# A gate map by 384 indirect transfers that add, in place of one-hot matmuls, and down loads eight tiles ahead

## The reference, cut to what matters

```python
v1, i1 = lax.top_k(s1, PEER_TOPK)            # 16 of 128 keys, per frame and head
v2, i2 = lax.top_k(s2, PEER_TOPK)
cand = (v1[..., :, None] + v2[..., None, :]).reshape(N, PEER_HEADS, 256)
cidx = (i1[..., :, None] * PEER_NKEYS + i2[..., None, :]).reshape(N, PEER_HEADS, 256)
sc, sel = lax.top_k(cand, PEER_TOPK)
eidx = jnp.take_along_axis(cidx, sel, axis=-1).reshape(N, 128)
gate = jax.nn.softmax(sc, axis=-1).reshape(N, 128)
...
a = jnp.einsum('nd,ned->ne', xk, u_emb[ek])
coef = jax.nn.gelu(a, approximate=False) * gk
return jnp.einsum('ne,ned->nd', coef, v_emb[ek])
```

## Time and profile before

| | |
|---|---|
| median of 3 runs | 2089.0 us (2085.16 to 2090.39) |
| profiled execution | 2082.26 us, of it the span 2080.4 us |
| mean granted TensorE clock | 0.962 |
| TensorE matmuls | 1855.5 us busy (89%) |
| VectorE, ScalarE, GpSimd | 1183.3, 667.3, 529.1 us busy |
| DMA | 337.63 MB, mean 162 GB/s |

### The profile page before, as it was taken

How to read it: one execution, slowest core, us unless ns; L and a number is a source line. 1 busy time by engine, 2 the same in 40 slices (tenths; PEclk the granted TensorE clock), 3 DMA queues, 4 the chain that set the end, 5 groups by cost and what they waited for, 6 DMA issues and landing times. The chain is left out here.

```text
span 2080.4 us, 24469 instructions
## 1 busy us (share of the span) xinstructions
PE 1855.5 (89%) x8991; PEld 1498.2 (72%) x8991; DVE 1183.3 (57%) x2275; ACT 667.3 (32%) x1004; POOL 529.1 (25%) x422
## 2 busy tenths in 40 slices
PE   5999999889995899999999999996987777888776
PEld 4867777667884788888888888885865655666655
DVE  3269746436999688882222223346755565665656
ACT  4332123333322246663222222331322222222223
POOL 4643200004444400000000000037643333334330
PEclk9999979999998999999999999998999999999998
DMA  4322100412332339898444454557767767777773
GB/s 136 91 61 65 44 1 1 160 43 86 97 92 86 103 96 234 212 237 224 150 141 146 142 153 144 184 210 245 268 237 250 250 238 259 249 254 262 253 256 130
DMA packets 241691, 337.63 MB, mean 162 GB/s; under 512 B 119857, under 2 KB 178609, under 8 KB 241473
## 3 DMA queue, kind: packets, MB, share of 16 engines
q1 hardware_dynamic: 219088, 269.60, 41.9%
q0 software_dynamic: 22528, 67.19, 9.7%
HBM read 282.19 MB, written 54.53 MB: 162 GB/s over the span
## 5 line engine op out<-in xcount | busy, mean ns | idle before, releaser
L344 PE MATMUL psum<-v_hi,c_hi 128*128 128x512 f32 x768 | 318.0, 414 | 125.5 <-DVE c_lo L1682 125.5
L344 PE MATMUL psum<-x_hi,ts_hi_u 128*128 128x512 f32 x1024 | 406.0, 396 | 22.2 <-DVE ts_lo_u L1157 18.9
L345 PE MATMUL psum<-x_lo,ts_hi_u 128*128 128x512 f32 x1024 | 402.2, 393 | 0.0
L346 PE MATMUL psum<-x_hi,ts_lo_u 128*128 128x512 f32 x1024 | 402.0, 393 | 0.0
L1919 POOL DMA_INDIRECT sparse_rows<-in_peer_v,sparse_v_row x128 | 141.4, 1105 | 988.2 <-PE psum L346 662.6
L1157 DVE TENSOR_TENSOR ts_lo_u<-ts_raw_u,ts_hi_u 128x1024 fp32r<-128x1024 f32 x117 | 158.1, 1352 | 370.7 <-ACT ts_hi_u L1152 370.4
L345 PE MATMUL psum<-v_lo,c_hi 128*128 128x512 f32 x768 | 309.5, 403 | 0.0
L346 PE MATMUL psum<-v_hi,c_lo 128*128 128x512 f32 x768 | 308.6, 402 | 0.0
L1819 ACT ACTIVATE v_hi<-v_raw 128x1024 fp32r<-128x1024 f32 x128 | 135.6, 1060 | 478.7 <-DMA v_raw<-in_peer_v 394.9
L344 PEld LDWEIGHTS psum<-v_hi,c_hi 128*128 128x128 f32 x768 | 150.4, 196 | 185.9 <-DVE c_lo L1682 155.1
L1680 DVE TENSOR_TENSOR v_lo<-v_raw,v_hi 128x1024 fp32r<-128x1024 f32 x128 | 156.6, 1223 | 205.1 <-ACT v_hi L1819 205.1
(11 more groups left out here) (231 smaller groups left out, 2624.0 us busy)
## 6 DMA issues: line engine op xcount, KB each, us to landing
ts_raw_u<-in_peer_u SPq DMA_DIRECT2D x128, 512.0 KB, 3.8
v_raw<-in_peer_v SPq DMA_DIRECT2D x128, 512.0 KB, 5.6
gate_map<-gate_stage SPq DMA_DIRECT2D x48, 512.0 KB, 5.7
up_acts<-ut_out_u SPq DMA_DIRECT2D x96, 192.0 KB, 1.9
act_in<-up_acts SPq DMA_DIRECT2D x96, 192.0 KB, 2.4
gate_in<-gate_map SPq DMA_DIRECT2D x96, 192.0 KB, 5.0
raw_in<-in_w_in SPq DMA_DIRECT2D x56, 256.0 KB, 2.8
ts_raw_wq<-in_peer_wq SPq DMA_DIRECT2D x16, 512.0 KB, 4.0
```

The source lines that it names most:

```text
L344: nc.tensor.matmul(out, l_hi, r_hi, start=first, stop=False)
L345: nc.tensor.matmul(out, l_hi, r_lo, start=False, stop=False)
L346: return nc.tensor.matmul(out, l_lo, r_hi, start=False, stop=last)
```

## The change

- `one_hots`, `split_gates`, `rows`, `copy_rows`, `store_gates` and their buffers go, and in routing the transposes with their copies.
- In routing `addresses(b)` gives, for each dense block, frame and slot, the cell of `gate_map`. SP stores zeros over the whole map, 32 stores of 128 x 1536 values, two behind each routing step; GpSimd clears the tile of zeros first.
- GpSimd's list in `experts` opens with 384 indirect transfers (`scatter_gate`): 128 gates each, one per frame, added to the map's cells by the DMA. Between two heads of a block it waits until the first has landed. The first `load_up_gate` waits for all of them.
- `RESIDENT` is 16 for 32: 16 more tiles are stored to `up_acts` and loaded again.
- The rings of `v_raw`, `act_in` and `gate_in` hold eight (`RAW`); `load_coef(e)` stands behind `load_v(e)`.
- Row additions begin at tile 10 and are spread evenly (`rows_by`); `gather_act` runs eight slots ahead of `gather_row`.
- TensorE's loop over the up tiles is one loop of equal bodies.

```diff
@@ -69,13 +69,12 @@
...
 ROUTE_TILES = 24
-RESIDENT = 32
+RESIDENT = 16
 DENSE_BLOCKS = NB - 1
...
+ZERO_COLS = 1536
+ZERO_STORES = P * DENSE // ZERO_COLS
@@ -1262,7 +1257,11 @@
...
+    def store_zeros(x):
+        sp.dma_start(gates_d.rearrange("e p f -> e (p f)")[:, x * ZERO_COLS:(x + 1) * ZERO_COLS], zeros[:]).then_inc(zeroed, 16)
...
+    sp.wait_ge(zeros_done, 1)
     for j in range(2, G + 2):
         load_q(j)
     for n in range(STEPS):
@@ -1271,6 +1270,8 @@
                 load_q(j + 2)
         for t in ups[n]:
             next_up(t)
+        for x in range(n * ZERO_STORES // STEPS, (n + 1) * ZERO_STORES // STEPS):
+            store_zeros(x)
...
         next_up(t)
@@ -1309,14 +1310,6 @@
     for b in range(NB):
         for x in range(SEL):
             up(sel_up + SEL * b + x)
-        if b >= DENSE_BLOCKS:
-            continue
-        pe.wait_ge(picked_done, b + 1)
...
-        nc.tensor.transpose(bank[:, 0:P], picked[:, b % 2, 0].rearrange(flat), ident[:])
-        nc.tensor.transpose(bank[:, P:2 * P], picked[:, b % 2, 1].rearrange(flat), ident[:])
-        nc.tensor.transpose(bank[:, 2 * P:3 * P], gates[:, b].rearrange(flat), ident[:]).then_inc(turned, 1)
@@ -1428,26 +1413,31 @@
...
     def sums(b):
-        if b >= 2:
-            dve.wait_ge(turned, b - 1)
         for t in range(2):
...
-        settle(nc.vector.tensor_reduce(frame[:], diag[:], AX.X, ALU.add))
...
+    def addresses(b):
...
+        if b >= DENSE_BLOCKS:
+            nc.vector.scalar_tensor_tensor(out=places["v_row"][:], in0=i1, scalar=float(NKEYS), in1=i2,
...
+        dve.wait_ge(placed, b + 1)
+        if b < DENSE_BLOCKS:
+            nc.vector.tensor_scalar(places["gate_at"][:, b], expert[:], float(DENSE), frame[:, b:b + 1],
+                                    ALU.mult, ALU.add)
+        else:
+            nc.vector.tensor_scalar(places["act_at"][:], expert[:], float(P), frame[:, 0:1], ALU.mult, ALU.add)
...
+    settle(nc.vector.tensor_reduce(frame[:, 0:1], diag[:], AX.X, ALU.add))
+    for b in range(1, NB):
+        nc.vector.tensor_scalar(frame[:, b:b + 1], frame[:, 0:1], float(P * b), None, ALU.add)
     for n in range(STEPS):
@@ -1478,18 +1468,20 @@
         for x in range(2, SEL + 1):
             low_u(sel_up + SEL * (b - 1) + x)
         sums(b - 1)
+        addresses(b - 1)
         low_u(sel_up + SEL * b + 1)
     for x in range(2, SEL):
         low_u(sel_up + SEL * (NB - 1) + x)
     sums(NB - 1)
...
-    sparse_places()
+    addresses(NB - 1)
...
+    nc.gpsimd.memset(zeros[:], 0.0).then_inc(zeros_done, 1)
     for j in range(2, G + 1):
@@ -1519,84 +1511,55 @@
     RING = 4
+    RAW = 8
...
+    FIRST_ROW = 10
@@ -1612,50 +1575,16 @@
+    def rows_by(e):
+        return min(SLOTS, max(0, e - FIRST_ROW) * SLOTS // (NKEYS - FIRST_ROW - RING))
@@ -1698,19 +1628,8 @@
         nc.vector.scalar_tensor_tensor(out=into, in0=dn.rows[:, r], scalar=dn.weight[:, j:j + 1], in1=into,
...
-    nc.vector.tensor_copy(gm.iota_b[:], iota[:])
-    split_gates()
...
     ut.split_lo(nc.vector, dve, R + 1, 1)
...
     for n in range(TILES):
-        if n < STEPS:
-            one_hots(n, n % 2)
         if n + 2 < TILES:
             ut.split_lo(nc.vector, dve, n + (R + 2), n % 2)
         if n >= FIRST_KEPT:
@@ -1721,18 +1640,13 @@
...
     for e in range(EARLY, NKEYS):
-        body, i = divmod(e, BODY)
         if e >= RESIDENT:
             product(e)
         low(e)
-        if body:
-            if i == 0:
-                weigh(body)
-            add_row(e)
-        elif i == BODY - 1:
-            weigh(0)
-            for j in range(BODY):
-                add_row(j)
+        for j in range(rows_by(e), rows_by(e + 1)):
+            if j % BODY == 0:
+                weigh(j // BODY)
+            add_row(j)
     dve.wait_ge(row_added, SLOTS)
@@ -1743,19 +1657,6 @@
...
-    def rows(n, par, first):
-        pe.wait_ge(hot_done, n + 1)
-        for r in range(STEP):
...
-            for x in range(PARTS):
-                last = nc.tensor.matmul(out, gm.one1[:, par, r], gm.val2[:, par, x, r], start=x == 0,
-                                        stop=x == PARTS - 1)
-            if at == BANKROWS - 1:
...
     def down(e, i, first, final):
         pe.wait_ge(c_lo_done, e + 1)
@@ -1768,19 +1669,9 @@
...
-    ut.product(nc, pe, x_hi, x_lo, R, 0, False)
-    for par in range(2):
-        ut.product(nc, pe, x_hi, x_lo, R + par + 1, 1 - par, False)
-        rows(par, par, par == 0)
-    with pe.Fori(1, STEPS // 2) as it:
+    with pe.Fori(0, TILES // 2) as it:
         for par in range(2):
-            ut.product(nc, pe, x_hi, x_lo, it * 2 + (R + par + 1), 1 - par, False)
-            rows(it * 2 + par, par, False)
-    with pe.Fori(STEPS // 2, TILES // 2 - 1) as it:
-        for par in range(2):
-            ut.product(nc, pe, x_hi, x_lo, it * 2 + (R + par + 1), 1 - par, False)
-    ut.product(nc, pe, x_hi, x_lo, R + TILES - 1, 1, False)
...
+            ut.product(nc, pe, x_hi, x_lo, it * 2 + (R + par), par, False)
@@ -1813,10 +1696,10 @@
     def split_down(e):
         i = e % RING
-        act.wait_ge(v_in[i], 16 * (e // RING + 1))
+        act.wait_ge(v_in[e % RAW], 16 * (e // RAW + 1))
         if e >= RING:
             act.wait_ge(down_done, e - RING + 1)
-        nc.scalar.activation(dn.v_hi[:, i], dn.v_raw[:, i], ACT.Copy).then_inc(v_hi_done, 1)
+        nc.scalar.activation(dn.v_hi[:, i], dn.v_raw[:, e % RAW], ACT.Copy).then_inc(v_hi_done, 1)
         if e < RESIDENT:
             act.wait_ge(kept, e + 1)
             nc.scalar.activation(dn.c_hi[:, i], dn.resident[:, e], ACT.Copy).then_inc(c_hi_done, 1)
@@ -1850,35 +1724,27 @@
...
-        if x == 0:
-            sp.wait_ge(staged, (ch + 1) * inner * banks)
-        i2 = slice(x * piece, (x + 1) * piece)
...
-                     gm.stage[:, ch % 2, i2]).then_inc(gates_stored[ch % 2], 16)
     def load_up_gate(n):
         k = kept_at(n)
         if k == 0:
-            for i in range(2):
-                sp.wait_ge(gates_stored[i], 16 * GATE_STORES // 2)
+            for b in range(DENSE_BLOCKS):
+                sp.wait_ge(scattered[b], 16 * SLOTS)
         if k >= 2:
             sp.wait_ge(kept, k - 1)
         sp.dma_start(dn.up_gate[:, k % 2], gates_d[R + n]).then_inc(up_gate_in[k % 2], 16)
     def load_v(e):
-        if e >= RING:
-            sp.wait_ge(v_lo_done, e - RING + 1)
-        sp.dma_start(dn.v_raw[:, e % RING], io["peer_v"][:, order[e]]).then_inc(v_in[e % RING], 16)
+        if e >= RAW:
+            sp.wait_ge(v_lo_done, e - RAW + 1)
+        sp.dma_start(dn.v_raw[:, e % RAW], io["peer_v"][:, order[e]]).then_inc(v_in[e % RAW], 16)
     def load_coef(e):
-        i = e % RING
-        if e - RESIDENT >= RING:
-            sp.wait_ge(coef_done, e - RESIDENT - RING + 1)
+        i = e % RAW
+        if e - RESIDENT >= RAW:
+            sp.wait_ge(coef_done, e - RESIDENT - RAW + 1)
@@ -1888,28 +1754,21 @@
         if FIRST_KEPT <= n + 1 < TILES:
             load_up_gate(n + 1)
         if n == LEAD - 2:
-            for e in range(RING):
+            for e in range(RAW):
                 load_v(e)
...
         ut.store(sp, acts_d, acts_s, R + n, n % 2)
     sp.wait_ge(ut.product_done, NKEYS)
     sp.dma_start(g_final[:], io["norm_final"][0:1, :].broadcast_to([P, D])).then_inc(g_final_in, 16)
-    for e in range(RING, NKEYS):
+    for e in range(RAW, NKEYS):
         load_v(e)
-        if RESIDENT <= e + RING < NKEYS:
-            load_coef(e + RING)
+        if e >= RESIDENT:
+            load_coef(e)
...
-    places = acts_s.rearrange("e p f -> (e p f)").unsqueeze(1)
+    gate_cells = gates_d.rearrange("e p f -> (e p f)").unsqueeze(1)
+    act_cells = acts_s.rearrange("e p f -> (e p f)").unsqueeze(1)
     def gather_row(j):
@@ -1918,24 +1777,42 @@
             pool.wait_ge(row_added, j - GATHERED + 1)
         nc.gpsimd.indirect_dma_start(
...
-            bass.IndirectOffsetOnAxis(sparse["v_row"][:, j:j + 1], 0)).then_inc(row_in[r], 16)
+            bass.IndirectOffsetOnAxis(places["v_row"][:, j:j + 1], 0)).then_inc(row_in[r], 16)
     def gather_act(j):
         nc.gpsimd.indirect_dma_start(
-            dn.picked[:, j:j + 1], None, places,
-            bass.IndirectOffsetOnAxis(sparse["act_at"][:, j:j + 1], 0)).then_inc(picked_in[j // BODY % 2], 16)
+            dn.picked[:, j:j + 1], None, act_cells,
+            bass.IndirectOffsetOnAxis(places["act_at"][:, j:j + 1], 0)).then_inc(picked_in[j // BODY % 2], 16)
+    def scatter_gate(b, j):
+        nc.gpsimd.indirect_dma_start(
+            gate_cells, bass.IndirectOffsetOnAxis(places["gate_at"][:, b, j:j + 1], 0),
+            gates[:, b].rearrange("p h k -> p (h k)")[:, j:j + 1], None, compute_op=ALU.add).then_inc(scattered[b], 16)
+    pool.wait_ge(zeroed, 16 * ZERO_STORES)
+    for h in range(PEER_HEADS):
+        for b in range(DENSE_BLOCKS):
+            if h:
+                pool.wait_ge(scattered[b], 16 * per_head * h)
+            for k in range(per_head):
```

(64 more changed lines are left out.)

149 lines of the change are left out of this document (31 added, 118 removed).

## The result

| | before | after |
|---|---|---|
| median of the runs | 2087.2 us (4 runs) | 2114.0 us (2110.6 to 2117.2, 4 runs) |
| span of the profiled execution | 2080.4 us | 2108.8 us |
| mean granted TensorE clock | 0.962 | 0.913 |

What follows compares the result with a forecast made beforehand. Matmuls were taken to bound the up stage, the latency of SP's queue loop the down stage. Terms -69 - 145 + 10 + 3 - 8 = -209 took 2082.3 to 1873 profiled, median 1878 us; range 1830 to 1995.

Steps and rivals of the forecast that it cites:

- the scatter's pace: GpSimd's 384 transfers in the up stage: 1.26 us each, costing +10 us; ends 0 and 137 (pace 1.60).
- 384P - 477: TensorE's stall in us in the up stage, for a transfer pace P; 7 us at 1.26.
- A wait of SP over 50 us: Sign of being wrong: SP waiting that long for the scatter, where a stall of 5 to 15 us was expected.
- Rival A: Scatter: the add is slow, 2.2 us a transfer, stall 368, median 2238 us; chance 0.11 (0.10 of it slower).
- the gain without the scatter: All terms but the scatter's: 219 us, so the kernel is slower once 384P - 477 exceeds that, from P = 1.81 us.
- size is no cost on GpSimd: Argument against A: the gather's issue takes 0.95 us whether a descriptor moves 4 B or 4 KB.
- Down stage: Nothing in SP's queue waits for the present tile and sparse_act waits go: -145 us; ends -172 and no gain.
- term of 4.32 us for a tile: Down stage: time for each of 112 coefficient-loading tiles at 349 GB/s; 4.08 for the 16 resident ones, 549 us together.
- Rival C: Down stage: DMA engines bind it, mean rate stays near 251 to 259 GB/s, no gain there, median 2024 us; chance 0.13.
- One-hots: Up stage: removing the one-hots and their 1152 matmuls gives -69 us; bounds -65 to -71.
- Zero stores: Routing: 32 stores of 786 KB on SP's queue cost +3 us; ends 0 and +15.
- Transposes: Routing: without them TensorE no longer waits for picked, -8 us; ends 0 and -12.

Runs made afterwards that it cites:

- two blocks: The changed kernel with gates scattered for two of the three dense blocks only (256 transfers), the third block's gates left out: 1877.7 us, ratio 0.8994.
- half the partitions: The changed kernel with its 384 transfers taking 64 partitions each instead of 128, the gates of half the frames left out: 2073.8 us.
- plain writes: The changed kernel with its 384 indirect transfers writing their gates instead of adding them: 2341.6 us, ratio 1.1216.
- rows half: The kernel before with only the spread row additions and activation gathers one body ahead, queue and rings as before: 2046.7 us, ratio 0.9815.
- queue half: The kernel before with rings of eight, 16 resident tiles and load_coef behind load_v, row additions and act gathers in their old order: 2021.0 us, ratio 0.969.
- The down part alone: The kernel before with rings of eight, 16 resident tiles, load_coef behind load_v, spread rows, acts gathered eight ahead, one-hots kept: 1926.9 us, ratio 0.9236.

## Why the prediction was wrong

*The step that failed* is the scatter's pace: "The nearest row is the gather of 128 values: start to start 1.26 us", and from it +10, with ends 0 and 137. It was 1.888 us, so 384P - 477 is 248, and SP's wait 251. The rest of that term held: the cover of 477 us, the place of the wait, and who stands behind it. By the up results TensorE's stall was 248 us in the change, 12 with two blocks, 209 with half the partitions and 227 with twelve resident tiles; the expression with each run's own pace (and 4 x 5.44 less for the twelve tiles) gives 248, 12, 208 and 227. A wait of SP over 50 us was one of the signs of being wrong that the prediction had named. The gather was the wrong nearest row because it lacks the add: take the add away and GpSimd needs 0.96 us again. The forecast's world as such, a scatter at that pace beside a TensorE at full speed, no run reached, because plain writes starve TensorE.

*Rival A* is what happened, and the pace went past its threshold of 1.81 us; its price (a second descriptor, 2.2 us) was too high, and which of its two reasons it is, no run shows. That the gain without the scatter came out at its 219 us (248 - 28.4) is luck: 22 us more in the down stage stand against as much in smaller misses. That "size is no cost on GpSimd" was no argument against it: the cost comes from the operation, and at least half of it is per transfer. The upper end of 1.60 us in the forecast was for a busy VectorE; an operation that no row shows should have had the doubled work as its end, inside the range.

*Down stage*, -145 forecast, -167 measured. The mechanism was right: SP's loop was the limit, ScalarE now waits for TensorE (284 us) instead of v_raw, the clock is 1.00. But the waits for sparse_act, told as a loss of 70 us beside the queue's, are a second limit just behind it: without the rows half the queue half gains 68 us only. The term of 4.32 us for a tile was mis-sized; the DMA engines hold 370 GB/s, above the 349 extrapolated from a share, and TensorE's own 4.08 is the pace, with the DMA engines just keeping up (share 1.01). Rival C fell with it. The Trainium skill's share of 358 GB/s for one core (HBM Reference, Specifications), which gave 4.21 us, was nearer than my 349 and still low: here, with the core alone, 370 were held.

*One-hots*, -69: right. The stretch from first to last up tile is 629.0 - 69 + 248 = 808, for 815 measured.

*The other 7 us* are a term that the prediction put at nothing without a reason. With rings of eight SP issues eight v loads at a stretch (4.90 us) ahead of an up tile's load; ScalarE then waits 7.27 us for `ts_raw_u`, and two up results come 8.8 and 8.7 us apart instead of 5.44 (1518.78, 1527.61, 1536.35). The down part alone and its queue half show the same two gaps; the rows half, with rings of four, does not.

*Zero stores*, +3 forecast, 9 measured, within the ends. *Transposes*, -8 forecast; 753.98 - 501.69 = 252.3 for 744.21 - 495.27 = 248.9 before makes routing 3.4 us longer, so with the 9 of the zeros they gave about 5.6, the address arithmetic taken off.

With the true pace the sum is 1873 + 238 = 2111, less 22 for the down stage, plus 6 and 2 for routing, 6 that was there before it, and 7 for the eight v loads: 2110 for 2110.7. The sign hung on one price that the trace did not have.

## What to carry to other kernels

An operation that no row shows (here the add in an indirect transfer) wants a price from both sides that reaches past the point where it decides the sign, however well a sibling without it is known; if only one thing can be measured beforehand, it is that. Work "on an idle engine" is free only up to the moment when a queue waits for its end: write the cover as count times pace less the time till that wait, and put the wait as late in the queue as it goes (5.2 us a tile here). Cut such a stream to what its cover holds: with the down part the same, all three blocks by the old way took 1926.9 us, all by the new way 2114.0, and two by the new and one by the old 1909.8. A fill that can stand in a stage where the DMA engines idle belongs there (9 us here).
